# One wide product for the high weights of gate and up in a mixture-of-experts loop

## The reference

```python
def expert_block(args):                       # rows of one expert
    xblk, e = args
    gu = xblk @ w_gu[e] + b_gu[e]             # 1024 -> 2048, gate and up interleaved
    gate = jnp.minimum(gu[:, ::2], 7.0)
    up = jnp.clip(gu[:, 1::2], -7.0, 7.0)
    act = (up + 1.0) * gate * jax.nn.sigmoid(1.702 * gate)
    return act @ w_down[e] + b_down[e]        # 1024 -> 1024
```

## Time and profile before

| | |
|---|---|
| time, median of 3 runs | 2753.58 us (2752.61 to 2753.84) |
| time of the profiled execution | 2729.14 us |
| span of the trace | 2727.3 us |
| mean granted clock of PE over the span | 0.971 |
| PE busy | 2489.2 us, 91% |
| weight loads (PEld) busy | 2167.1 us, 79% |
| VectorE busy | 1753.6 us, 64% |
| ScalarE busy | 1556.5 us, 57% |
| GpSimd busy | 800.1 us, 29% |
| read from HBM | 496.99 MB |

### The profile page before, as it was taken

The page is one execution under the profiler, slowest core; times in us unless marked ns, Lnnn a source line. Parts: engine busy times, 40 slices in busy tenths (PEclk is TensorE's granted clock), DMA queues, the critical chain, the costliest instruction groups (busy, mean ns, idle before and its releaser), DMA issues. The chain is left out here.

```text
span 2727.3 us, 135979 instructions
## 1 busy us (share of the span) xinstructions
PE 2489.2 (91%) x57293; PEld 2167.1 (79%) x57293; DVE 1753.6 (64%) x2056; ACT 1556.5 (57%) x1972; POOL 800.1 (29%) x627
## 2 busy tenths in 40 slices
PE   8999997999998966999999999999998999999993
PEld 2444554999996536989989899888998999999993
DVE  2424796666665775172555575787777776688883
ACT  3521552555555434173555575787777676678873
POOL 1301202677771122122222222322232323232321
PEclk9999998999999977999999999999999999999997
DMA  9601001011003238184565776998888977799966
GB/s 365 224 8 56 3 1 29 28 32 31 23 23 105 106 125 326 23 295 128 180 243 165 256 265 218 333 376 318 317 314 327 340 272 279 278 333 344 337 246 204
DMA packets 124489, 536.93 MB, mean 197 GB/s; under 512 B 12540, under 2 KB 13552, under 8 KB 91616
## 3 DMA queue, kind: packets, MB, share of 16 engines
q1 hardware_dynamic: 107120, 481.80, 46.7%
q0 software_dynamic: 14464, 47.79, 7.7%
q10 hardware_dynamic: 2832, 6.37, 0.6%
HBM read 496.99 MB, written 38.92 MB: 196 GB/s over the span
## 5 line engine op out<-in xcount | busy, mean ns | idle before, releaser
L2386 PE MATMUL ps<-qkv,weights 128*128 128x64 f16 x10496 | 935.8, 193 | 61.9 <-issue 24.3
L2386 PEld LDWEIGHTS ps<-qkv,weights 128*128 128x128 f16 x10496 | 921.2, 98 | 76.0 <-issue 37.9
L2388 PE MATMUL ps<-qkv,weights 128*128 128x64 f16 x10496 | 935.5, 193 | 2.7 <-issue 2.7
L2387 PE MATMUL ps<-qkv,weights 128*128 128x64 f16 x10496 | 935.4, 193 | 0.0
L2387 PEld LDWEIGHTS ps<-qkv,weights 128*128 128x128 f16 x10496 | 921.6, 98 | 2.1 <-issue 2.1
L2388 PEld LDWEIGHTS ps<-qkv,weights 128*128 128x128 f16 x10496 | 921.7, 98 | 0.3 <-issue 0.3
L1833 DVE SCALAR_TENSOR_TENSOR weights<-hT,weights 128x2048 f16<-128x2048 f16 (+1 forms) x256 | 588.2, 2350 | 159.4 <-ACT weights L1261 130.7
L1261 ACT ACTIVATE weights<-hT 128x2048 f16 (+1 forms) x256 | 526.7, 2098 | 75.9 <-DMA hT<-in_w_gu_dram 55.6
L2403 PE MATMUL ps<-qkv,weights 128*128 128x64 f16 x5248 | 472.9, 193 | 24.5 <-DVE weights L1838 22.2
L2403 PEld LDWEIGHTS ps<-qkv,weights 128*128 128x128 f16 x5248 | 461.7, 98 | 32.3 <-DVE weights L1838 27.8
L2404 PE MATMUL ps<-qkv,weights 128*128 128x64 f16 x5248 | 472.6, 193 | 0.0
(11 more groups left out here) (423 smaller groups left out, 4317.3 us busy)
## 6 DMA issues: line engine op xcount, KB each, us to landing
hT<-in_w_gu_dram SPq DMA_DIRECT2D x256, 1024.0 KB, 8.7
qkv<-in_w_down_dram SPq DMA_DIRECT2D x128, 1024.0 KB, 6.0
weights<-in_w_ada_dram SPq DMA_DIRECT2D x12, 2048.0 KB, 15.7
qkv<-in_w_in_dram SPq DMA_DIRECT2D x4, 2048.0 KB, 7.8
hT<-decay_rows SPq DMA_DIRECT2D x20, 256.0 KB, 3.3
hT<-beta_rows SPq DMA_DIRECT2D x20, 256.0 KB, 3.2
qkv<-in_x_dram ACTq DMA_DIRECT2D x8, 512.0 KB, 6.5
weights<-in_w_in_dram SPq DMA_DIRECT2D x2, 2048.0 KB, 14.2
```

Source lines behind the costliest of these rows:

```text
L2386: pe.matmul(dst, ghi[k][:, b, c], xT[:, 0, k, :], start=first, stop=False, skip_group_check=True)
L2387: pe.matmul(dst, ghi[k][:, b, c], xT[:, 1, k, :], start=False, stop=False, skip_group_check=True)
L2388: last = pe.matmul(dst, glo[k][:, b, c], xT[:, 0, k, :], start=False, stop=end, skip_group_check=True)
```

## The change

In `gate_up` on PE, the two products under the high weights (line 2386 with the high half of x, line 2387 with the low half) become one product whose moving operand is both halves of x, 2 x 64 = 128 columns. It writes two neighbouring groups of 64 columns in PSUM, so gate and up together take four banks, 0 to 3, instead of two. The product with the low weights (line 2388) still has 64 columns and adds into the first of the two groups. The first group then holds high x high + low x high, the second high x low, and the two have to be added.

VectorE does that in `read_gate_up`: its first add takes the first groups and the bias and writes `gate_up_n` as before; then it waits for its own result by the chain, and a second add takes `gate_up_n` and the second groups and writes `gate_up_n` again. The semaphore `s_gr`, which lets `swiglu` begin and lets PE overwrite the banks, is now raised by the second add. The chain has three links per block instead of two and is begun in `read_gate_up`. The other PSUM users of the loop move: x transposes from bank 2 to 6, `down` from 3 to 7; the result transposes stay in 4 and 5.

```diff
-        BG, BU, BX, BT, BY = 0, 1, 2, 3, 4
+        BG, BU, BX, BT, BY = 0, 2, 6, 7, 4
...
-            chain = Chain(dve, s_chain, 2)
+            chain = Chain(dve, s_chain, 3)
...
             def read_gate_up(t, e):
-                both = ps[:, BG:BG + 2, :].rearrange("p b (c t) -> p (b c) t", c=8)
+                both = ps[:, BG:BG + 4, :].rearrange("p b (c j t) -> p (b c) j t", c=4, j=2)
                 bias = btab.rearrange("p e j -> p (e j)")
                 dve.wait_ge(s_gu, t * GK + GK)
                 reached(dve, s_a, t, 1, 0)
-                dve.tensor_tensor(gate_up_n, both, bias[:, bass.ds(e * 16, 16)].unsqueeze(2).to_broadcast([P, 16, B]),
-                                  ALU.add).then_inc(s_gr, 1)
+                chain.turn(t)
+                chain(dve.tensor_tensor(gate_up_n, both[:, :, 0], bias[:, bass.ds(e * 16, 16)].unsqueeze(2).to_broadcast([P, 16, B]),
+                                        ALU.add))
+                dve.tensor_tensor(gate_up_n, gate_up_n, both[:, :, 1], ALU.add).then_inc(s_gr, 1)
 
             def swiglu(t):
-                chain.turn(t)
...
                     for f in range(8):
-                        dst, c = ps[:, bk, f * B:(f + 1) * B], slice(f * P, (f + 1) * P)
-                        first, end = k == 0 and f == 0, k == GK - 1
-                        pe.matmul(dst, ghi[k][:, b, c], xT[:, 0, k, :], start=first, stop=False, skip_group_check=True)
-                        pe.matmul(dst, ghi[k][:, b, c], xT[:, 1, k, :], start=False, stop=False, skip_group_check=True)
+                        at, c = f % 4 * 2 * B, slice(f * P, (f + 1) * P)
+                        first, end = k == 0 and f % 4 == 0, k == GK - 1
+                        both, dst = (ps[:, bk + f // 4, at:at + n * B] for n in (2, 1))
+                        pe.matmul(both, ghi[k][:, b, c], xT[:, :, k, :], start=first, stop=False, skip_group_check=True)
                         last = pe.matmul(dst, glo[k][:, b, c], xT[:, 0, k, :], start=False, stop=end, skip_group_check=True)
```

## The result

The changed kernel takes 2768.55 us (median of 4 runs, 2767.84 to 2770.49) against 2753.65 us before (2752.61 to 2753.84), a ratio of 1.0058 with an interval of 1.0043 to 1.0073 (ratios here and below are as on record; they differ a little from the quotient of the two medians, 1.0054 here). It is 14.9 us slower; the forecast said 10.9. The profiled execution of after took 2767.98 us with a span of 2766.2.

A forecast was written before the change was run, and what follows sets the result against it. PE was taken to bound plain blocks, VectorE's ordered queue the changes of expert. Switches +9.9, plain blocks -5.3, three-and-two cycles +3.1, two-block experts +3.5, last block -0.3: +10.9 on 2753.58 gives 2764.5 us; 8-in-10 range 2743 to 2780.

The forecast's parts named there:

- three-and-two cycles: Four later cycles of a three-block and a two-block expert: second adds ahead of low chunks cost +3.1 us together.
- two-block experts: Five two-block experts from 2456.80: the read ahead of the last four low chunks costs +3.5 us together.
- ahead of the loop, last block and end: Last block of the loop: PE's earlier down products cover the read ahead of the last ones; -0.3 us.
- The plain block: Block in the middle of a long expert: second add hidden, 18.75 us becomes 18.42; 16 x -0.33 = -5.3 us.
- rival of the slow product: Gate/up products on PE: the wide product runs at the pace of 81 ns, total about 3000 us; chance 2%.
- The second add: VectorE's read of PSUM: 1.22 us more, some 1.25 with its wait, per block; 103 us over 82 blocks.
- The first switch: Three blocks around the first one-block expert: about 65 us instead of 63.05; block behind gives back 0.8; net +1.1.
- Nine switches x 1.1 = +9.9: All nine changes with a one-block expert cost +1.1 us each through VectorE's queue; bounds -0.5 to +3.2 each.
- Read hidden: Rival at the switches: PE's gain is kept and the read hidden in VectorE's idle time; -19.5 us, 2734; chance 12%.
- transfers pace the switches: Rival: transfers absorb the reads at the switches, only plain blocks count; -5 to +2 us, about 2751; chance 17%.
- The clock: Rival: PE's longer idle time ahead of one-block experts drops the clock, nine falls at 1.7 us; 2780; chance 9%.
- the forecast's own signs of being wrong: Three blocks staying at 63 us, the clock falling at the switches, or the wide product taking over 60 ns.

The follow-up runs named there:

- the two narrow products: The kernel before without the product high weights x low x (line 2387), leaving 256 gate/up products of 64 columns per block; 2688.58 us on chip 1.
- the doubled read: The kernel before with its VectorE read of PSUM done twice, the second behind a wait on the first; 2786.06 us, ratio 1.0125, on chip 9.
- the kernel with two falls: The changed kernel with the read behind three low chunks of the next expert instead of four; 2770.96 us, ratio 1.0137, on chip 1.
- the one with twelve: The changed kernel with its read in halves, both adds and the clamp of gate first; 2767.79 us, ratio 1.0142, on chip 1.
- the wide product alone: The changed kernel without its second add, high weights x low x left out of the result; 2735.44 us, ratio 0.9941, on chip 9.
- the gate read first: The changed kernel with the direct release and its read in halves, gate first; 2728.94 us, ratio 0.9997, on chip 2.
- the direct release: The changed kernel with VectorE's last activation operation raising its semaphore itself, without waiting for its own result; 2739.03 us, ratio 1.0031, on chip 2.

## Why the forecast came out as it did

The two sums side by side, by the starts of the blocks. "Without pauses" is the first profile of before against the changed kernel on chip 2; "with pauses" is before on chip 9 against the profile after of the result.

| part | forecast | without pauses | with pauses |
|---|---|---|---|
| first two blocks | -0.7 (in plain) | -5.1 | -6.5 |
| 14 other plain blocks | -4.6 | -4.5 | -8.5 |
| nine cycles with a one-block expert | +9.9 | +24.3 | +19.3 |
| three-and-two cycles | +3.1 | +5.9 | +8.5 |
| two-block experts | +3.5 | +9.1 | +5.9 |
| ahead of the loop, last block and end | -0.3 | -0.9 | -0.7 |
| together | +10.9 | +28.8 | +17.9 |
| timed medians | | +27.3 | +14.9 |

**The plain block: right.** 18.43 us against a forecast of 18.42, and 10.88 for 10.87; 55.7 ns from DeltaNet's rows was the price of the wide product in the expert loop too. Where there are pauses the change takes most of them away as well, 0.61 a block in all; the profile that the forecast read has none, so it could not show this. The forecast's rival of the slow product is out: a wide and a narrow product, each with its load, take 85.0 ns together (10.88 us by 128). The figure of about 81 ns a product, quoted from the Trainium skill's page "TensorE: Matmul & The Clock Gate", section "Back-to-back issue gap", does not hold here.

**The second add: right.** 1221 ns for 1.22, VectorE busy 1853.0 for 1854.

**The first switch: right in place and size, with one step of the chain off.** On chip 2 the three blocks take 65.00 us (forecast about 65), and the block behind 19.25 instead of 19.95, 0.7 given back (forecast 0.8). PE idles 2.70 us ahead of the one-block expert (near 3 was forecast). VectorE's timeline there:

```profile
1195.69 1.22 DVE L1872 TENSOR_TENSOR qkv<-ps,same 128x1024 f32<-128x1024 f32 x1
1196.94 1.22 DVE L1874 TENSOR_TENSOR qkv<-qkv,ps 128x1024 f32<-128x1024 f32 x1
...
1200.90 9.13 DVE L1833 SCALAR_TENSOR_TENSOR weights<-hT,weights 128x2048 f16<-128x2048 f16 x4 [0.88 <-DVE qkv L1882]
1211.46 8.90 DVE L1838 SCALAR_TENSOR_TENSOR weights<-qkv,weights 128x2048 f16<-128x2048 f32 x4 [1.44 <-ACT weights L1267]
1220.28 1.22 DVE L1872 TENSOR_TENSOR qkv<-ps,same 128x1024 f32<-128x1024 f32 x1
1221.53 1.22 DVE L1874 TENSOR_TENSOR qkv<-qkv,ps 128x1024 f32<-128x1024 f32 x1
```

Measured from the start of the three blocks, the first read of these rows begins 1.3 us later than its like in the earlier trace rows, and the last read ends 2.5 later, as followed. In between, the four low chunks do not keep the 2.5: they begin at 43.0 us instead of 41.7, since the activation ahead of them waits 0.36 us for the Silu where it waited 1.57 before. The down chunks come 1.3 later by ScalarE, as forecast, so the end of the chain came out right all the same.

On the chip of the result the three blocks took 64.61 for 62.75, again +1.9, but the block behind 20.80 for 20.73: nothing came back.

**The term that was off most: one switch made the price of all nine.** "Nine switches x 1.1 = +9.9" was 24.3 without pauses. The nine fall into two groups. The five with plain blocks between them cost 1.3, 1.8, 2.1, 2.2 and 1.7 us, 1.8 in the mean: the 0.7 given back behind the first shrinks to 0.4 and then to nothing, and the one sampled was the cheapest. Of the four cycles of four blocks, which follow each other with no plain block between, three cost 5.4, 3.4 and 4.5, the last 1.8. In the first of them VectorE's eight low chunks, which showed no wait in the earlier trace rows and show none at this place in the kernel before (first row), no longer run through (the other rows, the changed kernel on chip 2):

```profile
1782.22 18.68 DVE L1833 SCALAR_TENSOR_TENSOR weights<-hT,weights 128x2048 f16<-128x2048 f16 x8 [0.88 <-DVE qkv L1881]
```

```profile
1784.32 14.27 DVE L1833 SCALAR_TENSOR_TENSOR weights<-hT,weights 128x2048 f16<-128x2048 f16 x6 [0.87 <-DVE qkv L1882]
1798.96 2.29 DVE L1833 SCALAR_TENSOR_TENSOR weights<-hT,weights 128x2048 f16<-128x2048 f16 x1 [0.36 <-ACT weights L1261]
1801.40 2.29 DVE L1833 SCALAR_TENSOR_TENSOR weights<-hT,weights 128x2048 f16<-128x2048 f16 x1 [0.15 <-ACT weights L1261]
1803.61 1.22 DVE L1872 TENSOR_TENSOR qkv<-ps,same 128x1024 f32<-128x1024 f32 x1
```

```profile
1796.67 2.11 ACT L1261 ACTIVATE weights<-hT 128x2048 f16 x1 [1.78 <-DMA hT<-in_w_gu_dram]
```

They wait for ScalarE, and ScalarE for a transfer that came late. These waits come to 0.5 us. Before them, the first four low chunks of the cycle already begin 6.55 us behind its start instead of 5.09 (1770.32 against 1763.77, and 1769.46 against 1764.37), again behind a wait for ScalarE. Together they make 2.0 of the 3.6 us by which this cycle is dearer than the five; the rest is not followed. That the late transfer is the delay of one cycle handed to the next through SP's queue fits the order of the code, but no run isolated it.

**The two-block experts: one term left out.** The forecast looked at the last four low chunks alone. But the read of the expert's first block ends 2.3 us later too: the second add of the block ahead holds back the four low chunks that stand before it, and it has a second add of its own. VectorE at that place, in the changed kernel on chip 2 and in the kernel before, and PE's first product behind it in each:

```profile
2485.67 8.89 DVE L1833 SCALAR_TENSOR_TENSOR weights<-hT,weights 128x2048 f16<-128x2048 f16 x4
2494.48 1.21 DVE L1872 TENSOR_TENSOR qkv<-ps,same 128x1024 f32<-128x1024 f32 x1
2495.72 1.22 DVE L1874 TENSOR_TENSOR qkv<-qkv,ps 128x1024 f32<-128x1024 f32 x1
```

```profile
2497.09 0.22 PE L2388 MATMUL ps<-qkv,weights 128*128 128x128 f16 x1 [1.61 <-DVE qkv L1874]
```

```profile
2464.16 8.89 DVE L1833 SCALAR_TENSOR_TENSOR weights<-hT,weights 128x2048 f16<-128x2048 f16 x4
2472.97 1.22 DVE L1871 TENSOR_TENSOR qkv<-ps,same 128x1024 f32<-128x1024 f32 x1
```

```profile
2475.57 0.19 PE L2386 MATMUL ps<-qkv,weights 128*128 128x64 f16 x1 [0.23 <-issue]
```

Before, the read was over 1.38 us ahead of PE's next block; now PE waits for it. The block went from 18.75 to 19.81 us, +1.06, at each of the nine two-block experts, those in the three-and-two cycles too: 9.5 us that no term of the sum held. Without it, the two-block experts cost 3.8 us against 3.5 forecast, and the three-and-two cycles 1.7 against 3.1 (whose own sum gives 3.0). The windows of before had room to show it: with 7.5 us from the last product to the next block, a read that ends 6.2 behind that product has 1.4 to spare, and 2.3 was put on it.

**The first two blocks: an effect of another kind.** 5 to 6.5 us came back at the second block, the gap shown with the two narrow products. The earlier trace rows began behind it and the forecast never looked.

**Why the total still came near.** It was luck: two errors of opposite sign. By the last column the changes of expert cost 33.7 us where 16.5 was forecast; the first two blocks and the pauses gave back 15.0 where 5.3 was forecast. That leaves 17.9 between two profiles and 14.9 between the medians. Adding a difference read on one kind of chip to a median of the other was the unseen risk; on chip 2 the same sum would have said 2742.7 where 2759.1 was measured.

**The rivals.** "Read hidden" and "transfers pace the switches" are refuted by the doubled read (+33.4). The clock: behind the first two blocks of the loop it fell seven times in the profile after and never in either profile of before. (At the start of the loop it is low in every profile, in the kernel before from 1055 to 1072 us.) So one of the forecast's own signs of being wrong, the clock falling at the switches, came true. On chip 2 one fall follows 3.28 us of idle PE; the windows before, in and behind it:

```profile
1803.00:1806.20 3.20, 0.00 (x0) 0.00 (x0) 3.13 (x4) 2.03 (x1) 0.00 (x0) 0.80 1.04 319
1806.30:1811.70 5.40, 5.40 (x69) 5.40 (x70) 4.17 (x5) 4.71 (x3) 0.00 (x0) 0.50 1.01 420
1811.80:1817.00 5.20, 5.20 (x126) 5.20 (x124) 5.20 (x3) 4.92 (x6) 1.74 (x1) 1.00 0.94 321
```

So the falls were foreseen, and their price of 1.7 us each was not borne out: the kernel with two falls and the one with twelve took the same time on the same chip, though they differ in VectorE's order too. And on chip 2 the first three one-block cycles, without a fall, cost 1.3, 1.8 and 2.1 us, and the next two, with one each, 2.2 and 1.7. A part for the longest falls can't be excluded.

## What to carry to other kernels

Where an engine's ordered queue sets the pace at some stages, price an edit at every place where something is queued behind it, and at several instances of each: the one switch that was followed well gave 1.3 where the mean of nine was 2.7. A trade of PE time for VectorE time is judged by the stage that binds, not by the engines' totals: on chip 9, 17 us of gain on PE's side was real, and so was twice that in reads. Look at what an engine waits for of its own first: here one wait of VectorE on its own last result, 0.8 us a block, was worth 16 us, about as much as the wide product alone (17.3, on chip 9), and cost nothing. An edit that shows nothing alone may still be worth making beside another, where two waits of one place overlap: the gate read first gave 10.1 us only once the direct release was in.

## What the runs showed of the hardware

The same kernel has two speeds by chip, 2732 and 2752 us, and part of the difference sits in PE's stream of products as pauses (the one shown 0.27 us), 0.33 us in a plain block, with the clock at 1.00 and nothing waited for. With the wide product, which takes a third of the gate/up products and loads out of the loop, they shrink to 0.10 us a block. On all three chips the loop with 384 products a block has 4.4 to 6.4 us of idle time of PE ahead of its second block, and those with 256, wide or narrow, have 1.1. The gap is put down to the number of PE instructions; that the pauses are of the same kind is a guess. How the instructions reach the engine no row shows, and it stays open.
